# A decoder layer with a mixture of experts: the first expert's rows marked, listed, gathered and turned in two halves of 128, ahead of TensorE's loops

## The chip, the cores and the metric

One core of a Trainium2 chip runs one launch of the whole layer in float32. The time is the device time of that launch in microseconds. A profiled execution gives a page and a trace; other executions give the times.

## What is computed

The reference is one decoder layer: a combined attention mixer (latent attention and a forgetting attention side by side), a cross-attention to 256 memory tokens, a mixture of experts, and a last RMSNorm. Only the last but one bears on the change:

```python
xt = hn.reshape(T, D)                                   # T = 1024 tokens, D = 1024
logits = (xt @ w_router) + b_router                     # 32 experts
top_vals, top_idx = lax.top_k(logits, TOP_K)            # 4 of 32
gates = jax.nn.softmax(top_vals, axis=-1)
flat_e = top_idx.reshape(-1)
order = jnp.argsort(flat_e)
tok = order // TOP_K
xs = xt[tok]                                            # rows grouped by expert
h = lax.ragged_dot(xs, w_gate_up, group_sizes) + b_gate_up[e_sorted]
...                                                     # clamped SwiGLU
y = lax.ragged_dot(act, w_down, group_sizes) + b_down[e_sorted]
out = jax.ops.segment_sum(y * gate, tok, num_segments=T)
```

## The kernel before

The kernel is written per engine: each engine has its own stream of instructions, and semaphores order them. TensorE (PE) multiplies and transposes, VectorE (DVE) scales, adds and compares, ScalarE (ACT) does activations, GpSimd (POOL) issues the indirect DMAs, and SyncE (SP) issues the plain loads and stores.

**Router.** Tiles of 128 tokens pass the cross-attention and the router. For each, DVE picks the four largest logits and adds to `sel` (128 x 8 x 32, a 1 where a token has chosen an expert). After the last tile DVE raises `r_chosen` to SELECTED (1), PE multiplies ones and prefix matrices with the choices (`r_rank` 1 and 2), and DVE makes from this `key`, the place of each token within each expert's list. The experts are ordered by falling number of tokens. PE multiplies once more (`r_rank` 3), and DVE writes `items` (the expert of each place in the order, and its size) and `bounds` (how many experts are larger than each class width), and raises `r_chosen` to LISTED (3).

**Listing an expert.** For item i, DVE compares each tile's keys with a row of 256 numbers: eight instructions (`hots`, L2281) give `hot`, 128 x 8 x 256, a one-hot matrix from token to place. PE's `e_index` multiplies `hot` with `mv`, which holds each token's number in two parts, 8 products for places 0 to 127 and 8 for 128 to 255, into four columns of PSUM bank `pt[0]`. DVE's `indices` copies them (`ix`, L2287), adds the two parts to row numbers (`gidx`, L2290), raises `e_idx`, and forms the same numbers for the later scatter (`ixs`). Places beyond the expert's size get a number over the limit and are left out.

**Gathering.** POOL's `gather` (L955) waits for `e_idx` and issues two indirect DMAs of 128 rows of 4 KB, from the normed rows in HBM (`d_xn`) into `xg`; both count on `e_xg`.

**Turning in.** PE's `e_turn_in` waits for both halves (`e_xg` at 32 for item 0), and transposes `xg` in four groups g, each of four 128 x 128 blocks: two blocks of columns times two halves of rows. Groups use the banks `pt[0]` and `pt[1]` in turn; DVE's `x_copies` (L1938) scales each filled bank into `xe_t` and frees it, and raises `e_xt` after the last.

**PE's loops.** The experts fall into six classes by size (widths 256, 208, 184, 160, 144, 128), with one body of code for each. `up_to` (L1914 to L1924) nests five loops of two passes, each with a test `at < end` (loops L1916, tests L1917); `item` is the body. Only the number in `bounds` tells how many items a class has, so that an empty class is jumped over at run time. Each item begins with a test `at < 1` (L1909): item 0 alone runs its own turn-in there, as all later items are turned in by the item before. Then `whole` waits for `e_xt` and runs the products for gate and up (`e_gate_up`), the listing of the next item, the transposes of the last item's output, and the products for down. The kernel needs 32 items.

**Order around the change, PE:** wait for LISTED; load two item sizes and five bounds into registers (L1850, L1886), with `e_index(0)` between the third bound and the fourth; wait for ACT's biases (`r_ex` 3) and transpose them (eight blocks, L1892); set `at` to 0 (L1896); enter the loops; turn in item 0 inside the first item. **DVE:** load the first expert's number (L2277); `hots(0)`; `indices(0)`; gates (L2319 to L2326, `r_gate`); `x_copies(0)`; `hots(1)`; first item. **POOL:** `gather(0)`, then the splitting of the biases into three parts (L966 to L981), `gather(1)`, and the loop of shares, gathers and scatters. **SP:** loads the first weights (slot 0, 2 MB) once LISTED is reached; then waits for the gather (L769), stores the gates (L770), loads slot 1, waits for the store, and loads slots 2 to 5 (L603).

The lines in the profile are often those of helpers: L1376 is every product, L1760 the transposes of the turn-in, L603 every load. "DVEq" or "PEq" is an engine's sequencer, which runs branches, register work and waits.

Of the kernel before, what the change touches and what calls it, by code (L numbers as in the profile page):

```python
# [78 lines left out]
def build(nc, S, a, out):  # L79
    T, D, NT, KD, H, FW, E, CAP = S.T, S.D, S.NT, S.KD, S.H, S.FW, S.E, S.CAP  # L80
    ctx = ExitStack()
    with ctx:
        def sem(name):
            return ctx.enter_context(nc.semaphore(name))
# [362 lines left out]
        def index_use(i):  # L447
            return e_pt[0].base + 3 * i + 1
# [112 lines left out]
        def nothing():  # L561
# [5 lines left out]
            sem("r_ss"), sem("r_rstd"), sem("r_rnt"), sem("r_chosen"), sem("r_ex"), sem("r_rn"))  # L567
        SELECTED, PLACED, LISTED = 1, 2, 3
        r_st = sem("r_st")
        r_rank = sem("r_rank")  # L570

        e_w = [Handoff(sem, f"e_w{c}") for c in range(SLOTS)]
        e_hot = sem("e_hot")
        e_idx = sem("e_idx")
        e_xg = sem("e_xg")
# [12 lines left out]
        def apart(eng):  # L588


            eng.sem_inc(passed, 1)
# [9 lines left out]
        def _(sp):  # L601
# [165 lines left out]
            load(slots[0][:, :, :], expert_part(0, first), e_w[0].full)  # L767
            sp.wait_ge(e_xg, 32)
            sp.wait_ge(r_gate, 1)  # L769
# [41 lines left out]
        def _(po):  # L811
# [149 lines left out]
            po.wait_ge(r_ex, 1)  # L961
            gather(0)

# [401 lines left out]
        def _(pe):  # L1365
# [360 lines left out]
            def if_second(n, yes, no):  # L1726
# [5 lines left out]
                with pe.Else():  # L1732
                    no()

            def e_index(i, n=None):

                pe.wait_ge(e_hot, i + 1)

                pe.wait_ge(e_pt[0].free, index_use(i))

                def tokens(hb, tiles):
                    return product(pt[0][:, hb * 2:hb * 2 + 2],
                                   [(hot[:, t, hb * P:(hb + 1) * P], mv[:, t, :]) for t in range(tiles)])

                tokens(0, NT)
                if_second(n, lambda: tokens(1, NT).then_inc(e_pt[0].full, 1),
                          lambda: tokens(1, 1).then_inc(e_pt[0].full, 1))

            def e_turn_in(i, groups, n=None):

                pe.wait_ge(e_xg, 32 * (i + 1))
                for g in groups:
                    b, k = g % 2, g // 2 + 1
                    pe.wait_ge(e_pt[b].free, turn_in_use(b, i, k))

                    def blocks(halves):
                        for j in range(4):
                            if j % 2 in halves:
                                c = 2 * g + j // 2
                                m = pe.transpose(pt[b][:, j * P:(j + 1) * P], xg[:, j % 2, c * P:(c + 1) * P], ident)  # L1760
                        m.then_inc(e_pt[b].full, 1)

                    if_second(n, lambda: blocks((0, 1)), lambda: blocks((0,)))
# [118 lines left out]
            below = []  # L1882
            for c in range(S.CLASSES - 1):
                if c == 3:
                    e_index(0)
                below.append(pe.value_load(bounds[0:1, c:c + 1], min_val=0, max_val=E))  # L1886
            below.append(E)
            pe.wait_ge(r_ex, 3)
            for b in range(2):
                pe.wait_ge(e_rows[b].free, e_rows[b].base + 1)  # L1890
                for m in range(4 * b, 4 * b + 4):
                    x = pe.transpose(wide[1][0:BP, m * P:(m + 1) * P],  # L1892
                                     b_thrice[:, m, :], ident)
                x.then_inc(e_rows[b].full, 1)
            at = pe.alloc_register("item_at")
            pe.reg_mov(at, 0)  # L1896
# [3 lines left out]
            def item(w):  # L1900
# [7 lines left out]

                with pe.If_lt(at, 1):  # L1909
                    e_turn_in(0, range(4))  # L1910
                whole(i, i - 1, w, n_before, later, look_ahead)
# [23 lines left out]
        def _(ve):  # L1935
# [348 lines left out]
            def indices(i, e):  # L2284
# [5 lines left out]
                ve.scalar_tensor_tensor(out=gidx[:, :], **ids).then_inc(e_idx, 1)  # L2290
                ve.scalar_tensor_tensor(out=ixs[:, 0:2], **ids)
                ve.drain()
# [20 lines left out]
            first = expert_at(0)  # L2313
            hots(0, first)
            indices(0, first)
            ve.tensor_copy(ixp[:, :], ixs[:, :])

# [210 lines left out]
```

## Time and profile before

| | us |
|---|---|
| median of 3 runs | 2709.58 |
| lowest and highest run | 2707.89, 2711.74 |
| the profiled execution, its own time | 2707.28 |
| span of the profiled execution, first to last instruction | 2705.4 |

| engine | busy us | share | instructions |
|---|---|---|---|
| PE | 2638.0 | 98% | 17206 |
| DVE | 1091.5 | 40% | 2701 |
| ACT | 627.4 | 23% | 1386 |
| POOL | 379.9 | 14% | 391 |

The span is what the trace covers; 1.9 us of the execution lie outside it. All positions below are microseconds from the span's start. The mixer, cross-attention and router end at about 1070, and the 32 items of the expert stage fill the rest. A group of instructions in a timeline gives its start, the time that it covers, and in brackets how long the engine had been idle before it and what ended that. The profile counts one float32 product of the expert stage as two records, and a transpose as one.

### The profile page before, as it was taken

To read this page: it belongs to the slowest core of one execution; us is meant where nothing else is said; L and a number is where in the kernel's file an instruction comes from. 1 tells how busy PE (TensorE), PEld (TensorE's weight loads), DVE (VectorE), ACT (ScalarE), POOL (GpSimd) and SP (SyncE) were. 2 spreads that over 40 slices of the span, in tenths; PEclk is the share of its full clock that TensorE was granted. 3 is DMA by queue.
4 is the path that set the end of the run, shared out by engine and by line. 5 is a ranking of instruction groups with operands and counts; after the bars stand their busy time and mean duration, and the time that the engine had idled before them with its cause. 6 is when DMAs were issued, how large, how long until landed. Compare 5 with 4: busy or idle time off the path is not lost.

```text
span 2705.4 us, 49571 instructions
## 1 busy us (share of the span) xinstructions
PE 2638.0 (98%) x17206; PEld 2118.7 (78%) x17207; DVE 1091.5 (40%) x2701; ACT 627.4 (23%) x1386; POOL 379.9 (14%) x391
## 2 busy tenths in 40 slices
PE   9999999999999998999999999999999999999997
PEld 8455556666477774999999999998878787878785
DVE  1111145554212324433333344344455454545455
ACT  0333355553011112011111111111212121221212
POOL 0100022221000001111111111111111111112111
PEclk9999999999999998999999999999999999999998
DMA  8111243232300002765667677787888888888885
GB/s 293 47 51 54 64 151 90 79 116 92 129 1 9 31 31 103 303 209 194 221 218 254 225 276 260 269 274 264 318 299 319 301 310 306 312 297 312 300 310 202
DMA packets 108856, 533.95 MB, mean 197 GB/s; under 512 B 24290, under 2 KB 59042, under 8 KB 84208
## 3 DMA queue, kind: packets, MB, share of 16 engines
q1 hardware_dynamic: 88016, 498.99, 50.2%
q0 software_dynamic: 20768, 33.97, 5.7%
q8 instruction: 48, 0.79, 0.1%
q14 instruction: 24, 0.20, 0.0%
HBM read 506.64 MB, written 60.52 MB: 210 GB/s over the span
## 4 chain that ended last, share of the span: by engine, by line
PE 92%; DVE 3%; issue 2%; DMA 2%; ACT 1%; DVEq 1%; POOL 0%; ACTq 0%; POOLq 0%
PE bank L1376 45%; PE wide L1376 9%; PE wide L1836 9%; PE wide L1804 9%; PE bank L1426 8%; PE bank L1369 4%; PE wide L1500 2%; PE bank L1556 2%; PE bank L1760 2%; PE wide L1517 1%; DMA d_sum<-y_sb,sidx 1%; PE wide L1369 1%; DVE biased L2060 1%; DVE prob_t L2071 1%; ACT prob L1151 0%
## 5 line engine op out<-in xcount | busy, mean ns | idle before, releaser
L1376 PE MATMUL bank<-xe_t,slot 128*128 128x128 f32 (+4 forms) x8192 | 1025.2, 287 | 12.3 <-issue 11.2
L1376 PEld LDWEIGHTS bank<-xe_t,slot 128*128 128x128 f32 x8192 | 1014.5, 192 | 14.1 <-issue 13.7
L2336 DVE TENSOR_SCALAR glu<-bank,b_gu 128x256 f32<-128x256 f32 x256 | 123.8, 484 | 657.2 <-PE bank L1376 657.1
L1317 ACT ACTIVATE sig<-glu 128x256 f32<-128x256 f32 x256 | 106.7, 417 | 837.8 <-DVE glu L2336 835.5
L1836 PE MATMUL wide<-slot,act_t 128*128 128x512 f32 x608 | 267.8, 593 | 1.0 <-DVE act_t L2348 1.0
L1804 PE MATMUL wide<-act_t,slot 128*128 128x144 f32 (+3 forms) x1664 | 235.5, 302 | 0.0
L1804 PEld LDWEIGHTS wide<-act_t,slot 128*128 128x128 f32 x1664 | 231.8, 190 | 0.0
L1426 PE MATMUL bank<-w_in,xt 128*128 128x512 f32 (+1 forms) x512 | 217.6, 575 | 1.6 <-DVEq L1978 1.6
L1836 PEld LDWEIGHTS wide<-slot,act_t 128*128 128x128 f32 x608 | 112.5, 190 | 128.8 <-issue 126.2
L1334 ACT ACTIVATE y_t<-wide,b_dn 128x256 f32<-128x256 f32 x248 | 102.0, 471 | 421.2 <-PE wide L1836 212.9
L955 POOL DMA_INDIRECT xg<-d_xn,gidx x66 | 66.6, 1009 | 862.8 <-DVE gidx L2290 814.0
L1426 PEld LDWEIGHTS bank<-w_in,xt 128*128 128x128 f32 x512 | 94.8, 190 | 100.5 <-issue 100.5
L987 POOL DMA_INDIRECT share<-d_gate,sidx x64 | 67.8, 1059 | 458.6 <-DVEq L2357 415.4
L2348 DVE TENSOR_TENSOR act_t<-lin,sig 128x256 f32<-128x256 f32 x256 | 108.8, 425 | 41.0 <-issue 7.3
L1938 DVE TENSOR_TENSOR xe_t<-bank,gains 128x512 f32<-128x512 f32 x132 | 85.2, 686 | 96.8 <-PE bank L1760 91.6
L2338 DVE TENSOR_SCALAR lin<-bank,b_gu 128x256 f32<-128x256 f32 x256 | 121.6, 475 | 0.0
L2345 DVE TENSOR_TENSOR lin<-lin,glu 128x256 f32<-128x256 f32 x256 | 108.9, 425 | 19.4 <-issue 0.3
L1376 PEld LDWEIGHTS bank<-hn_t,w_xq 128*128 128x128 f32 x1024 | 115.5, 192 | 1.4 <-issue 1.1
L1376 PE MATMUL bank<-hn_t,w_xq 128*128 128x128 f32 x1024 | 115.7, 275 | 0.3 <-issue 0.3
L1376 PE MATMUL wide<-vw,px_t 128*128 128x512 f32 x256 | 112.4, 593 | 0.6 <-DVE lg_now L2171 0.6
L997 POOL DMA_INDIRECT d_sum<-y_sb,sidx x62 | 99.0, 1598 | 44.3 <-ACTq L1299 29.4
L1369 PE MATMUL bank<-const,prob 128*128 128x128 f32 x576 | 88.2, 281 | 11.6 <-DVE prob_t L2071 5.1
(302 smaller groups left out, 2455.6 us busy)
## 6 DMA issues: line engine op xcount, KB each, us to landing
slot<-in_w_gu SPq DMA_DIRECT2D x128, 2048.0 KB, 8.8
slot<-in_w_dn SPq DMA_DIRECT2D x64, 2048.0 KB, 7.7
w_in<-in_w_in SPq DMA_DIRECT2D x1, 6144.0 KB, 25.3
w_mem_k<-in_w_mem_kv SPq DMA_DIRECT2D x4, 1024.0 KB, 11.0
w_mem_v<-in_w_mem_kv SPq DMA_DIRECT2D x1, 4096.0 KB, 20.6
x_sb<-in_x SPq DMA_DIRECT2D x8, 512.0 KB, 3.3
cneg<-d_cneg SPq DMA_DIRECT2D x8, 512.0 KB, 6.6
d_vw<-mix_out SPq DMA_DIRECT2D x16, 256.0 KB, 2.2
```

Of the source, the lines that this page charges most:

```text
L997: po.indirect_dma_start(out=d_sum, out_offset=bass.IndirectOffsetOnAxis(ap=sidx[:, hb:hb + 1], axis=0), in_=y_sb[:, hb, :], in_offset=None ...
L1317: ac.activation(sig[m % 2][:, :], glu[m % 2][:, :], ACT.Sigmoid, scale=1.702).then_inc(e_sig, 1)
L1334: x = ac.activation(y_t[:, m, :], pp2[b][:, (m % 2) * CAP:(m % 2 + 1) * CAP], ACT.Identity, bias=b_dn[:, bass.ds(e * KD + m, 1)])
L1369: m = pe.transpose(dst[0:s.shape[-1], j * P:j * P + s.shape[0]], s, idn)
L1376: m = pe.matmul(dst, l, r_, start=(k == 0), stop=(k == n - 1))
L1426: m = pe.matmul(pp[b][:, 0:c1 - c0], xt[:, kk, :], w_in[:, kk, c0:c1], start=kk == 0, stop=kk == KD - 1)
L1804: x = pe.matmul(pp2[b][:, (m % 2) * CAP:(m % 2) * CAP + w], slots[4 + m // 4][:, k, (m % 4) * P:(m % 4 + 1) * P], act_t[:, k, 0:w], start= ...
L1836: x = pe.matmul(wide[1][:, hd * 512:(hd + 1) * 512], act_t[:, k, 0:P], slots[4 + hd][:, k, :], start=k == 0, stop=False)
L2336: ve.tensor_scalar(glu[b][:, :], pp[b][:, 0:CAP], b_gu[:, bass.ds(e * 2 * KD + 2 * m, 1)], 7.0, ALU.add, ALU.min).then_inc(e_glu, 1)
L2338: ve.tensor_scalar(lin[b][:, :], pp[b][:, CAP:2 * CAP], b_gu[:, bass.ds(e * 2 * KD + 2 * m + 1, 1)], 7.0, ALU.add, ALU.min).then_inc(e_gu[ ...
L2345: ve.tensor_tensor(lin[b][:, :], lin[b][:, :], glu[b][:, :], ALU.mult)
L2348: ve.tensor_tensor(act_t[:, m, :], lin[b][:, :], sig[b][:, :], ALU.mult).then_inc(e_act, 1)
```

## The change

The first item is taken out of the common path. DVE marks, copies and adds it in two halves of 128 places; PE multiplies the first half into bank `pt[1]` after its second bound (before: all after the third), and the second half into `pt[0]` after its third. POOL gathers each half once its numbers are there, on semaphores of their own (`e_half`, `e_xg`). PE transposes the first half of groups 0 and 1 when the first half has landed, the second half of both when the second has landed, then groups 2 and 3 as before, all in front of the loops and behind the bias transposes. The test `at < 1` and the turn-in go out of the items of all six classes. `r_chosen` gets two more steps and `r_rank` one. Waits for `e_xg` count 16 less for every item, since item 0's first half no longer counts there.

```diff
--- before.py
+++ after.py
@@ -565,12 +565,14 @@
         BIAS_ROWS = 2
         r_ss, r_rstd, r_rnt, r_chosen, r_ex, r_rn = (
             sem("r_ss"), sem("r_rstd"), sem("r_rnt"), sem("r_chosen"), sem("r_ex"), sem("r_rn"))
-        SELECTED, PLACED, LISTED = 1, 2, 3
+        SELECTED, PLACED, LISTED, HALF_HOT, HALF_LISTED = 1, 2, 3, 4, 5
+        HALF_MULTIPLIED = 4
         r_st = sem("r_st")
         r_rank = sem("r_rank")
 
         e_w = [Handoff(sem, f"e_w{c}") for c in range(SLOTS)]
         e_hot = sem("e_hot")
+        e_half = sem("e_half")
         e_idx = sem("e_idx")
         e_xg = sem("e_xg")
         e_y = Handoff(sem, "e_y")
@@ -765,7 +767,8 @@
             sp.wait_ge(r_chosen, LISTED)
             first = expert_of(0)
             load(slots[0][:, :, :], expert_part(0, first), e_w[0].full)
-            sp.wait_ge(e_xg, 32)
+            sp.wait_ge(e_half, 16)
+            sp.wait_ge(e_xg, 16)
             sp.wait_ge(r_gate, 1)
             sp.dma_start(d_gate.rearrange("(t p e) o -> p t (e o)", p=P, e=E), part[:, :, :]).then_inc(s_st, 16)
             load(slots[1][:, :, :], expert_part(1, first), e_w[1].full)
@@ -959,7 +962,19 @@
 
             po.wait_ge(r_st, 16 * NT)
             po.wait_ge(r_ex, 1)
-            gather(0)
+
+            def gather_half(hb, landed):
+                po.indirect_dma_start(
+                    out=xg[:, hb, :], out_offset=None, in_=d_xn,
+                    in_offset=bass.IndirectOffsetOnAxis(ap=gidx[:, hb:hb + 1], axis=0),
+                    bounds_check=T - 1, oob_is_err=False).then_inc(landed, 16)
+
+            po.wait_ge(r_chosen, HALF_LISTED)
+            apart(po)
+            gather_half(0, e_half)
+            po.wait_ge(e_idx, 1)
+            apart(po)
+            gather_half(1, e_xg)
 
 
 
@@ -1732,6 +1747,10 @@
                 with pe.Else():
                     no()
 
+            def tokens_of(bank_of, at_col, hb, tiles):
+                return product(bank_of[:, at_col:at_col + 2],
+                               [(hot[:, t, hb * P:(hb + 1) * P], mv[:, t, :]) for t in range(tiles)])
+
             def e_index(i, n=None):
 
                 pe.wait_ge(e_hot, i + 1)
@@ -1739,8 +1758,7 @@
                 pe.wait_ge(e_pt[0].free, index_use(i))
 
                 def tokens(hb, tiles):
-                    return product(pt[0][:, hb * 2:hb * 2 + 2],
-                                   [(hot[:, t, hb * P:(hb + 1) * P], mv[:, t, :]) for t in range(tiles)])
+                    return tokens_of(pt[0], hb * 2, hb, tiles)
 
                 tokens(0, NT)
                 if_second(n, lambda: tokens(1, NT).then_inc(e_pt[0].full, 1),
@@ -1748,7 +1766,7 @@
 
             def e_turn_in(i, groups, n=None):
 
-                pe.wait_ge(e_xg, 32 * (i + 1))
+                pe.wait_ge(e_xg, 32 * i + 16)
                 for g in groups:
                     b, k = g % 2, g // 2 + 1
                     pe.wait_ge(e_pt[b].free, turn_in_use(b, i, k))
@@ -1881,8 +1899,14 @@
 
             below = []
             for c in range(S.CLASSES - 1):
+                if c == 2:
+                    pe.wait_ge(r_chosen, HALF_HOT)
+                    pe.wait_ge(e_pt[1].free, e_pt[1].base + 1)
+                    tokens_of(pt[1], 0, 0, NT).then_inc(r_rank, 1)
                 if c == 3:
-                    e_index(0)
+                    pe.wait_ge(e_hot, 1)
+                    pe.wait_ge(e_pt[0].free, index_use(0))
+                    tokens_of(pt[0], 2, 1, NT).then_inc(e_pt[0].full, 1)
                 below.append(pe.value_load(bounds[0:1, c:c + 1], min_val=0, max_val=E))
             below.append(E)
             pe.wait_ge(r_ex, 3)
@@ -1892,6 +1916,20 @@
                     x = pe.transpose(wide[1][0:BP, m * P:(m + 1) * P],
                                      b_thrice[:, m, :], ident)
                 x.then_inc(e_rows[b].full, 1)
+            def turn_half(g, hb):
+                for j in (hb, hb + 2):
+                    c = 2 * g + j // 2
+                    m = pe.transpose(pt[g][:, j * P:(j + 1) * P], xg[:, hb, c * P:(c + 1) * P], ident)
+                return m
+
+            pe.wait_ge(e_half, 16)
+            for g in range(2):
+                pe.wait_ge(e_pt[g].free, turn_in_use(g, 0, 1))
+                turn_half(g, 0)
+            pe.wait_ge(e_xg, 16)
+            for g in range(2):
+                turn_half(g, 1).then_inc(e_pt[g].full, 1)
+            e_turn_in(0, (2, 3))
             at = pe.alloc_register("item_at")
             pe.reg_mov(at, 0)
             LEVELS = 5
@@ -1906,8 +1944,6 @@
                     pe.reg_mov(held, later)
                     pe.reg_mov(held_later, rows_in(i + 2))
 
-                with pe.If_lt(at, 1):
-                    e_turn_in(0, range(4))
                 whole(i, i - 1, w, n_before, later, look_ahead)
                 pe.reg_mov(at, i + 1)
 
@@ -2288,7 +2324,11 @@
                 ve.drain()
                 ids = dict(in0=ix[:, :, 0], scalar=float(8 * T), in1=ix[:, :, 1], op0=ALU.add, op1=ALU.add)
                 ve.scalar_tensor_tensor(out=gidx[:, :], **ids).then_inc(e_idx, 1)
-                ve.scalar_tensor_tensor(out=ixs[:, 0:2], **ids)
+                token_rows(e)
+
+            def token_rows(e):
+                ve.scalar_tensor_tensor(out=ixs[:, 0:2], in0=ix[:, :, 0], scalar=float(8 * T), in1=ix[:, :, 1],
+                                        op0=ALU.add, op1=ALU.add)
                 ve.drain()
                 ve.scalar_tensor_tensor(out=ixs[:, 2:4], in0=ixs[:, 0:2], scalar=float(E),
                                         in1=iota[:, bass.ds(e, 1)].to_broadcast([P, 2]), op0=ALU.mult, op1=ALU.add)
@@ -2311,8 +2351,28 @@
 
 
             first = expert_at(0)
-            hots(0, first)
-            indices(0, first)
+            def half_hots(hb):
+                for t in range(NT):
+                    ve.tensor_scalar(hot[:, t, hb * P:(hb + 1) * P], iota[:, hb * P:(hb + 1) * P], shift[:, 0:1],
+                                     key[:, t, bass.ds(first, 1)], ALU.add, ALU.is_equal)
+
+            def rows_of_half(hb):
+                return ve.scalar_tensor_tensor(out=gidx[:, hb:hb + 1], in0=ix[:, hb, 0:1], scalar=float(8 * T),
+                                               in1=ix[:, hb, 1:2], op0=ALU.add, op1=ALU.add)
+
+            half_hots(0)
+            ve.drain().then_inc(r_chosen, 1)
+            ve.wait_ge(r_rank, HALF_MULTIPLIED)
+            ve.tensor_copy(ix[:, 0, :], pt[1][:, 0:2])
+            ve.drain()
+            rows_of_half(0).then_inc(r_chosen, 1)
+            half_hots(1)
+            ve.drain().then_inc(e_hot, 1)
+            ve.wait_ge(e_pt[0].full, index_use(0))
+            ve.tensor_copy(ix[:, 1, :], pt[0][:, 2:4]).then_inc(e_pt[0].free, 1)
+            ve.drain()
+            rows_of_half(1).then_inc(e_idx, 1)
+            token_rows(first)
             ve.tensor_copy(ixp[:, :], ixs[:, :])
 
             ve.wait_ge(r_ex, 2)
```

## Rows read from the trace of the kernel before

**Rows 1.** The page: busy time and share, and the chain's shares by engine.

```profile
PE 2638.0 (98%) x17206; PEld 2118.7 (78%) x17207; DVE 1091.5 (40%) x2701; ACT 627.4 (23%) x1386; POOL 379.9 (14%) x391
...
PE 92%; DVE 3%; issue 2%; DMA 2%; ACT 1%; DVEq 1%; POOL 0%; ACTq 0%; POOLq 0%
```

**Rows 2.** Chain of waits in order of time: start us, us, what.

```profile
1076.83 0.58 PE bank L1376 x16
...
1078.94 1.43 POOL xg L955
...
1080.68 4.70 DMA xg<-d_xn,gidx
...
1090.61 47.43 PE bank L1376 x272
```

**Rows 3.** PE's sequencer by line: count, ns min/median/max, first and last start.

```profile
L1886 PEldq TENSOR_LOAD <-bounds x5: 295/306/309, 1074.8 to 1077.5; - x5
...
L1896 PEldq MOVE  x1: 35/35/35, 1078.3 to 1078.3; - x1
...
L1917 PEldq COMPARE_BRANCH  x1: 4747/4747/4747, 1078.5 to 1078.5; - x1
...
L1917 PEldq COMPARE_BRANCH  x7: 65/65/4747, 1078.5 to 1085.2; - x7
...
L1901 PEldq FUSED_REGOPS  x1: 111/111/111, 1085.4 to 1085.4; - x1
...
L552 PEldq COMPARE_BRANCH  x1: 4821/4821/4821, 2687.2 to 2687.2; - x1
...
L1901 PEldq FUSED_REGOPS  x1: 110/110/110, 1235.4 to 1235.4; - x1
...
L1909 PEldq COMPARE_BRANCH  x32: 78/209/350, 1085.5 to 2640.4; - x32
```

**Rows 4.** Timeline of SP at the gather's landing: start us, us, line, op.

```profile
1085.39 0.38 SPq L770 DMA_DIRECT2D d_gate<-part  x1
```

**Rows 5.** Timeline of DVE, 1066 to 1090.

```profile
1066.11 0.29 DVE L2187 TENSOR_TENSOR eq<-const,idxf 128x128 f32<-128x128 f32 x1
...
1073.90 2.67 DVE L2281 TENSOR_SCALAR hot<-const,shift,key 128x256 bf16<-128x256 f32 x8 [1.13 <-issue]
...
1077.70 0.16 DVE L2290 SCALAR_TENSOR_TENSOR gidx<-ix 128x2 int32<-128x2 f32 x1
...
1078.79 0.42 DVE L2319 TENSOR_TENSOR part<-part,sel 128x256 f32<-128x256 f32 x1
...
1089.64 0.69 DVE L1938 TENSOR_TENSOR xe_t<-bank,gains 128x512 f32<-128x512 f32 x1 [0.16 <-PE bank L1760]
```

**Rows 6.** Timeline of POOL; and all gathers of L955, issue to landing.

```profile
1078.94 1.43 POOL L955 DMA_INDIRECT xg<-d_xn,gidx  x1 [13.70 <-issue]
...
1080.68 0.99 POOL L955 DMA_INDIRECT xg<-d_xn,gidx  x1 [0.30 <-issue]
...
DMA to landing us min/median/max: 2.1/5.2/15.8
```

**Rows 7.** Timeline of PE: turn-in, first products of items 0 and 1.

```profile
1085.76 3.84 PE L1760 MATMUL bank<-const,xg 128*128 128x128 f32 x16 [5.55 <-DMA xg<-d_xn,gidx]
...
1090.61 13.17 PE L1376 MATMUL bank<-xe_t,slot 128*128 128x208 f32 x64 [1.01 <-DVEq L2305]
...
1162.13 11.42 PE L1376 MATMUL bank<-xe_t,slot 128*128 128x208 f32 x64
```

**Rows 8.** PE at a change of class; its waits for issue (total, times, longest).

```profile
1236.15 11.91 PE L1376 MATMUL bank<-xe_t,slot 128*128 128x184 f32 x64 [2.39 <-issue]
...
PE bank L1376 <- issue: 11.2, 4, 3.3
```

**Rows 9.** Windows: from:to us, busy PE, PEld, DVE, ACT, POOL, PEclk, DMA share, GB/s.

```profile
1090.00:1095.00 5.00, 4.39 (x16) 4.31 (x16) 4.14 (x7) 0.00 (x0) 3.39 (x3) 0.60 0.99 423
...
1237.00:1241.00 4.00, 4.00 (x17) 4.00 (x16) 0.00 (x0) 0.00 (x0) 0.00 (x0) 0.57 1.00 430
```

## The prediction

> **What bounds the kernel now.** The page comes first: PE is busy for 98% of the span, and 92% of the chain that ended last is PE [rows 1]. A microsecond taken from another engine counts only where PE stands still. The chain in order of time shows where that is around the change: between the router and the first expert product PE waits for a string of small steps, namely marking on DVE, 16 narrow products, the row numbers, the gather on POOL, its landing, 16 transposes and their copies, and at 1090.61 the first product [rows 2]. From there PE runs on, so what this stretch gains or loses is gained or lost at the end.
>
> The chain names the gather's landing as what PE waited for. The next view, PE's sequencer by source lines, says more. PE set its loop register (L1896) at 1078.3 and came to the item's own register work (L1901) at 1085.4, 7.1 us later, and the first transpose started at 1085.76 [rows 3, 7]. SP, which waits for the same landing, issued its store at 1085.39 [rows 4]. So **two things ended within 0.3 us of each other**: the gather, and PE's way into five nested loops. Of those 7.1 us one branch took 4747 ns: the first test of L1917, which jumps over the nest of the 256-wide class, empty here since the first products are 208 wide. PE's one other jump over a body that never ran (L552, at the end) took 4821 ns; the seven tests of L1917 at the entry have a median of 65 [rows 3]. I read the two as the price of a jump into code that was not at hand.
>
> **First half (marked, listed, gathered).** Eight markings of 256 columns take 2.67 us, so 0.32 apart from start to start; a 128-column DVE instruction is 0.13 shorter than a 256-column one (0.29 against 0.42) [rows 5]. Eight half markings: 8 x 0.19 = 1.5 us, done at 1075.5. PE is later: it now waits between its second and third load of a bound; the five loads began from 1074.8 to 1077.5, so some 0.68 apart, and two end at 1076.1 [rows 3]. Eight products instead of 16 (0.58, rows 2) take 0.4: 1076.6. The copy and the sum end 0.45 after the products (1077.41 to 1077.86 before) [rows 2, 5]: 1077.05, **0.8 earlier**. POOL starts a gather 1.08 after the row numbers end (1078.94) and its two took 1.43 and 0.99 [rows 6]: it starts at 1078.1 and ends by 1079.5.
>
> **Second half.** DVE marks it only after the first half's sums: 1077.05 + 1.5 + 0.1 = 1078.7, PE's eight products to 1079.15 (PE's third load is hidden beside the marking), row numbers at 1079.6, POOL 1.08 later at 1080.7. Before, it started at 1080.68 [rows 6]: **nothing gained**. This gather landed 4.7 after its start [rows 2], 1085.4 at the latest; the fastest of all 66 gathers took 2.1 [rows 6], 1082.8 at the earliest. It meets the weight load of slot 0 as before, but most of the first half is out of its way: I take 1085.1, near the nearest row.
>
> The Trainium skill (DMA: Bandwidth & Descriptors, "Anatomy of one DMA") has about 2.0 us plus bytes over 436 GB/s for such a transfer. For the second half's 57 to 80 rows of 4 KB that is an estimate of 2.6 us, a landing at 1083.3 and a sum 1.8 us lower than mine; the row above, 4.7, is far from it.
>
> **Turn-in.** Before, from 1085.73 to 1090.61: four groups of four transposes, 16 in 3.84 (about 0.21 apart, 0.42 each), each group followed by a copy of 0.69, two banks [rows 2, 5, 7]. After, half of groups 0 and 1 is done early, in idle time. From 1085.2: group 0 is full at 1085.85, its copy to 1086.55, group 2's transposes to 1087.7; group 1's copy to 1087.2, group 3's transposes start at 1087.5 and end at 1088.6, the last copy at 1089.35, drained 1089.4. Against 1090.38 **1.0 us earlier**.
>
> **Loop entry.** The turn-in now stands in front of the loops, so that PE's sequencer begins the entry only when group 3 can start, at 1087.4. The 7.1 us stood beside the gather before, and that cover is gone. What is left as cover is the copies, to 1089.4. 1087.4 + 7.1 = 1094.5, and from L1901 on a change of class takes 0.75 to the product (1235.4 to 1236.15), 0.48 without the removed branch [rows 3, 8]: **the first product at 1095.0, 4.4 us later than 1090.61**. With the landing at 1082.8 or 1085.4 this term is 2.1 or 4.7.
>
> The Trainium skill (Runtime: NRT & Kernel Launch, "Instruction fetch mechanics") says that a taken branch to a target outside the fetched window stalls until the page is fetched. It gives PE room for 2048 instructions, by which a jump over one item's body (under 900) might find its target; by that the entry would take about 2.4 instead of 7.1, and the sum would be that of the first rival. The 4747 ns argue against it here.
>
> **Removed branch.** Each item loses the test L1909 (median 209 ns, 32 times). Inside a class it costs nothing: PE's queue covers it (PE waited for "issue" four times only, all at changes of class [rows 8]); if that cover were gone it would come back with at most 0.27 an item. At the four changes of class PE stood still for 11.2 us in all, 2.39 at the first [rows 8]; there the branch and its step of 0.06 lie on the path, 4 x 0.27 = 1.1 by the median, 4 x 0.41 = 1.65 by the longest (350 ns): I take **1.35 us gained**, between the two.
>
> **Clock.** PE's clock was at its lower level, 1.2 GHz, until about 1094.0, 3.4 us into the products; that cost 13.17 - 11.42 = 1.75 us over the first 64 product records against the same ones of the next item [rows 7, 9] (the mean of 0.60 from 1090 to 1095 is 4 us at a half and 1 at full). PE will now stand some 6 us between transposes and products instead of 1.0. Bounds: the slow part as short as 2.5 us (-0.45) or twice as long (+1.75); I take +0.8, nearer the middle. Two of the four class changes were followed by such a dip, the one at 1237 stands in [rows 9], about 1.7 each: none or four afterwards, 3.4 either way, taken as 0.
>
> **At nothing:** the eight bias transposes (L1892) move 2 us later into PE's wait for the gather, and ACT's copies and POOL's bias work behind them; first wanted by item 0's sixth step, 30 us on. DVE's token rows and gates end at some 1082.4, while SP waits for the gather until 1085. POOL's new wait has only the gathers behind it. SP's store and slots 1 to 5 go out 0.3 earlier; slot 1 is wanted 12 us after the first product, and the loads keep that margin.
>
> **Sum:** +4.4 - 1.35 + 0.8 = **+3.85 us**. The profiled execution took 2707.28, 2.3 below the median of 2709.58; from it 2711.1, by the median **2713.4**. A measurement of this kernel tells some 0.2%, 5.4 us, from no change, so this is likeliest "same".
>
> **Rivals.**
> *No stall at the new place* (0.17). For it: the first change of class leaves and enters five levels within the 2.39 us of its gap and PE's queue. Against: both jumps of the trace over a body never run stalled alike. Entry 7.1 - 4.7 = 2.4; the first product at 1090.3, and -0.3 - 1.35 gives -1.65, with no clock term: 2707.9.
> *A second stall, slower* (0.15). Place: between the turn-in and the first product. The weight loads of slots 1 to 5 now run at full rate when the code is fetched, or the 208-wide entry starts near the end of a fetched piece. Price: one more 4.75, so +8.6, 2718.2. It decides once the entry takes over 8.7 us instead of 7.1.
> *The intended gain* (0.05): early landing at 1082.8 and no stall: the first product about 1088, -2.6 - 1.35 = -4: 2705.6. Against it: the second gather starts no earlier.
>
> My forecast has 0.63, its own range 2710.5 to 2717. Over 5.4 slower: all but a little of the second rival and 0.14 of my own case (clock, landing at the late end): 0.28. Over 5.4 faster needs the third rival or the first, with both dips gone: 0.05. Range 2706.5 to 2718.5: from the first rival less its spread to the second with its own.
>
> **What would show it.** L1917's first test at over 4 us, but now behind the last transposes, and PE's idle row before the first 208-wide product at about 5.5 us, released by "issue". The first gather starting near 1078.1, the second near 1080.7. Gaps at class changes shorter by 0.3 each. I am wrong if that first test takes under 1 us, if the idle row names the DVE copies, or if the second gather lands before 1083.5.

## The result, and the profile after

| | before | changed |
|---|---|---|
| median, us | 2708.38 (20 runs) | 2712.57 (20 runs) |
| lowest and highest run | 2704.89, 2711.74 | 2709.47, 2714.71 |
| span of the profiled execution | 2705.4 | 2711.7 |

The ratio is 1.0014, 95% interval 1.0008 to 1.0020: the changed kernel is 4.2 us slower by the medians, 2.2 to 5.4 by the interval. 2713.4 had been forecast.

Positions in two executions can only be compared from a common event, since the router in front ended 3.3 us later in the profiled execution of the changed kernel, and in the profiled executions of the kernels below it ended anywhere between 1072.6 and 1076.2. I count from LISTED, the end of DVE's write of `bounds`. Timeline of DVE, before:

```profile
1072.62 0.15 DVE L2273 CAST bounds<-wide 128x5 int32<-128x5 f32 x1
```

and after, with the two half markings:

```profile
1075.89 0.15 DVE L2309 CAST bounds<-wide 128x5 int32<-128x5 f32 x1
...
1077.18 2.14 DVE L2356 TENSOR_SCALAR hot<-const,shift,key 128x128 bf16<-128x128 f32 x8 [1.14 <-issue]
...
1080.14 2.46 DVE L2356 TENSOR_SCALAR hot<-const,shift,key 128x128 bf16<-128x128 f32 x8
```

LISTED is at 1072.77 before and at 1076.04 after. The first half's eight markings took 2.14 us, the second half's 2.46; all eight whole ones took 2.67 [rows 5]. Timeline of POOL, the gathers (2 lines), and of SP, the store that goes out on the landing:

```profile
1081.30 1.28 POOL L967 DMA_INDIRECT xg<-d_xn,gidx  x1 [12.80 <-issue]
...
1084.42 0.98 POOL L967 DMA_INDIRECT xg<-d_xn,gidx  x1 [1.83 <-DVE gidx L2360]
```

```profile
1088.78 0.38 SPq L773 DMA_DIRECT2D d_gate<-part  x1
```

From LISTED the first gather starts at 5.26 (before 6.17), the second at 8.38 (7.91), and the landing shows at 12.74 (12.62) [rows 4, 6]. The gather in halves brings the rows in no earlier. What comes next stands in the chain of waits in order of time:

```profile
1084.42 4.29 DMA xg<-d_xn,gidx
...
1088.75 0.70 PE bank L1922 x2
...
1090.32 1.96 PE bank L1778 x8
...
1092.29 0.69 DVE xe_t L1974
...
1093.04 6.82 issue
```

The copies end at 1092.98, and then there are 6.82 us of "issue", in which PE's engine waits for nothing but its own sequencer. The sequencer's lines, with the columns of [rows 3]:

```profile
L1934 PEldq MOVE  x1: 35/35/35, 1090.8 to 1090.8; - x1
...
L1953 PEldq COMPARE_BRANCH  x1: 6334/6334/6334, 1091.0 to 1091.0; - x1
...
L1953 PEldq COMPARE_BRANCH  x7: 65/65/6334, 1091.0 to 1099.3; - x7
...
L1939 PEldq FUSED_REGOPS  x1: 133/133/133, 1099.5 to 1099.5; - x1
```

The register before the loops (L1934, L1896 before) is set at 1090.8, behind the turn-in. The first test (L1953, L1917 before) takes 6334 ns against 4747 [rows 3], the item begins at 1099.5, and the first product at 1099.87. PE's timeline, first products and the four changes of class:

```profile
1099.87 13.94 PE L1391 MATMUL bank<-xe_t,slot 128*128 128x208 f32 x64 [7.61 <-issue]
...
1245.82 10.24 PE L1391 MATMUL bank<-xe_t,slot 128*128 128x184 f32 x64 [2.05 <-issue]
...
1376.05 8.96 PE L1391 MATMUL bank<-xe_t,slot 128*128 128x160 f32 x64 [2.41 <-issue]
...
1547.40 9.77 PE L1391 MATMUL bank<-xe_t,slot 128*128 128x144 f32 x64 [2.78 <-issue]
...
1856.54 7.41 PE L1391 MATMUL bank<-xe_t,slot 128*128 128x128 f32 x64 [2.37 <-issue]
```

Against 17.84 us after LISTED [rows 7], the first product comes at **23.83: 6.0 later**. Its 64 records take 13.94 instead of 13.17 [rows 7]. The gaps at the changes of class are 2.05, 2.41, 2.78 and 2.37. Before, the first was 2.39 [rows 8] and the others were these:

```profile
1368.52 8.96 PE L1376 MATMUL bank<-xe_t,slot 128*128 128x160 f32 x64 [2.87 <-issue]
...
1540.37 9.78 PE L1376 MATMUL bank<-xe_t,slot 128*128 128x144 f32 x64 [3.28 <-issue]
...
1850.02 7.41 PE L1376 MATMUL bank<-xe_t,slot 128*128 128x128 f32 x64 [2.70 <-issue]
```

The sum falls from 11.24 to 9.61. The page's product row says the same of the wait for "issue", first before, then after:

```profile
L1376 PE MATMUL bank<-xe_t,slot 128*128 128x128 f32 (+4 forms) x8192 | 1025.2, 287 | 12.3 <-issue 11.2
...
L1391 PE MATMUL bank<-xe_t,slot 128*128 128x128 f32 (+4 forms) x8192 | 1024.2, 287 | 17.2 <-issue 17.2
```

Idle time for "issue" went from 11.2 to 17.2 us: 7.6 new ones before the first product, 1.6 fewer at the changes of class. Windows of the changed kernel behind the first and the third change (the third number from the end is the granted clock):

```profile
1245.82:1249.82 4.00, 4.00 (x26) 4.00 (x27) 0.00 (x0) 0.00 (x0) 0.00 (x0) 1.00 0.86 336
...
1547.40:1551.40 4.00, 4.00 (x21) 4.00 (x22) 0.00 (x0) 0.00 (x0) 0.00 (x0) 0.64 0.95 410
```

Behind the third change the clock fell to its lower level for 3.4 us, as before; behind the first it did not, where before it had [rows 9].

Ledger from LISTED: +5.98 to the first product, +0.77 for slower first products, -1.63 at the changes of class, and -1.67 because the records after the first change took 10.24 instead of 11.91 [rows 8], at the higher clock: +3.45. From LISTED to the end the two executions differ by 3.0, so 0.4 us are not accounted for.

### The profile page after: what moved, and what is told of

Its sections match the earlier page's. It is cut to its first block, busy times and chain, and to the rows that moved or that the text cites. A ratio compares the mean times of both kernels' runs of the same rounds, so it can differ in the third digit from the quotient of the medians.

```text
span 2711.7 us, 49522 instructions
## 1 busy us (share of the span) xinstructions
PE 2640.4 (97%) x17206; PEld 2119.7 (78%) x17207; DVE 1097.2 (40%) x2711; ACT 627.8 (23%) x1386; POOL 380.1 (14%) x391
## 4 chain that ended last, share of the span: by engine, by line
PE 93%; DVE 3%; issue 2%; DMA 1%; ACT 1%; DVEq 1%; ACTq 0%; POOL 0%; POOLq 0%
PE bank L1391 46%; PE wide L1391 9%; PE wide L1854 9%; PE wide L1822 9%; PE bank L1441 8%; PE bank L1384 4%; PE wide L1515 2%; PE bank L1571 2%; PE bank L1778 1%; PE wide L1532 1%; PE wide L1384 1%; DVE biased L2096 1%; DMA d_sum<-y_sb,sidx 1%; DVE prob_t L2107 0%; ACT prob L1166 0%
## 5 line engine op out<-in xcount | busy, mean ns | idle before, releaser
L1391 PE MATMUL bank<-xe_t,slot 128*128 128x128 f32 (+4 forms) x8192 | 1024.2, 287 | 17.2 <-issue 17.2
```

Source lines behind the costliest of these rows:

```text
L1391: m = pe.matmul(dst, l, r_, start=(k == 0), stop=(k == n - 1))
```

## The experiments

Theory A: the loss is the entry into the loops, with its jump over the empty class, which lost the gather as its cover. Theory B: the halving costs, with its second marking, second wait and second gather. Each time is against runs of the kernel before on the same chip. "Product" is the first product after LISTED in the profiled execution. "Low stretches" counts, in the same execution, the stretches of some 3.4 us behind a change of class in which the granted clock was at its lower level, 1.2 GHz.

| run | product, us | first 64 records | low stretches | median us | before | ratio, 95% interval |
|---|---|---|---|---|---|---|
| before | 17.84 | 13.17 | 2 | 2708.38 | | 1 |
| changed | 23.83 | 13.94 | 1 | 2712.57 | 2708.38 | 1.0014 (1.0008 to 1.0020) |
| hoist_only | 24.68 | 13.74 | 1 | 2711.89 | 2708.70 | 1.0009 (1.0000 to 1.0018) |
| turn_inside | 20.77 | 13.73 | 2 | 2710.08 | 2708.70 | 1.0004 (0.9995 to 1.0013) |
| before_no_empty | 17.65 | 13.65 | 2 | 2708.00 | 2708.70 | 0.9996 (0.9987 to 1.0005) |
| after_no_empty | 17.10 | 14.05 | 1 | 2704.15 | 2708.70 | 0.9985 (0.9976 to 0.9994) |
| loads_later | 21.44 | 13.44 | 1 | 2707.69 | 2708.30 | 0.9995 (0.9986 to 1.0004) |
| hoist_no_empty | 17.10 | 11.52 | 1 | 2704.58 | 2708.30 | 0.9986 (0.9977 to 0.9995) |
| two_paths | 17.91 | 13.79 | 1 | 2704.80 | 2708.30 | 0.9986 (0.9977 to 0.9996) |
| jump_first | 18.88 | 13.14 | 2 | 2708.35 | 2708.30 | 1.0001 (0.9992 to 1.0010) |
| two_empty | 35.63 | 13.26 | 1 | 2723.99 | 2708.74 | 1.0055 (1.0041 to 1.0068) |
| hoist_two_paths | 17.69 | 13.08 | 1 | 2704.75 | 2708.74 | 0.9985 (0.9976 to 0.9994) |

The two kernels of the change have 20 times each, the runs 11, two_empty 5.

**The low stretches follow the removed test.** The four kernels that keep a test at each change of class, in the items or in front of the nests, stand still there for 10.87 to 11.32 us in all and have two such stretches; the eight without it stand still for 9.59 to 9.66 us and have one. Each stretch costs 1.67 us over the 64 records behind the change (11.91 against 10.24 behind the first, 10.63 against 8.96 behind the second, 9.77 against 8.10 behind the third). With one profiled execution of each kernel this is a clean split of twelve; no run changes the gaps and nothing else, so why one stretch goes is not shown.

### hoist_only: one part of the change, on the kernel before

```diff
+            e_turn_in(0, range(4))
             at = pe.alloc_register("item_at")
...
-                with pe.If_lt(at, 1):
-                    e_turn_in(0, range(4))
```

> The kernel before with one edit: item 0's turn-in, whole and not in halves, stands in front of the loops, and the test at < 1 goes out of the items. Theory A (the loop entry with its jump over the empty class lost its cover): the jump starts only when the last group can be transposed, some 15.4 us after LISTED (in the kernel before 5.7), takes 4.7 to 6.3 us, and the first product comes 5 to 7 us later than before; the class changes give 1.4 to 1.6 back and the clock costs 0.8: 4.5 to 6.5 us slower than before. Theory B (the loss comes from the halving, with its second marking and second gather, and the hoist is what gains): faster than before by 1 to 2 us.

Timeline and sequencer of PE (the whole loop nest's first test is listed under L1916 here):

```profile
L1916 PEldq COMPARE_BRANCH  x1: 6339/6339/6339, 1089.4 to 1089.4; - x1
...
1098.28 13.74 PE L1376 MATMUL bank<-xe_t,slot 128*128 128x208 f32 x64 [7.95 <-issue]
```

Without any halving the jump takes 6339 ns and the product comes 6.8 us later than before; the median is 3.2 us up, less than the 4.5 to 6.5 expected: the missing low stretch, 1.7 us, was not in that sum. Theory B said faster, and it falls. The product is 0.9 us later than in the changed kernel: the jumps are alike (6339 and 6334 ns), so the halves seem to save that much here.

### turn_inside: the changed kernel without the hoist

```diff
                 with pe.If_lt(at, 1):
+                    pe.wait_ge(e_half, 16)
+                    ...                        # the turn-in in halves, as in the change
+                    e_turn_in(0, (2, 3))
                 whole(i, i - 1, w, n_before, later, look_ahead)
```

> The changed kernel with the turn-in (in halves) and the test at < 1 back inside the first item; listing and gathering stay in halves. Theory A: the jump starts once the second half's products and the last two bounds are through, 8.0 us after LISTED, and the entry's 7.1 us end at some 15.3, after the landing at 12.6; the turn-in starts there, first product 19.8 to 20.2 us after LISTED (before 17.8, changed 23.8): 2 us slower than before, and 1.5 to 3 faster than the changed kernel. Theory B: as slow as the changed kernel or slower, since the halves are kept and the tests come back.

PE: the jump, the last two groups of the turn-in, the first products.

```profile
L1954 PEldq COMPARE_BRANCH  x1: 4536/4536/4536, 1084.5 to 1084.5; - x1
...
1091.61 1.94 PE L1922 MATMUL bank<-const,xg 128*128 128x128 f32 x8 [5.41 <-issue]
...
1096.95 13.73 PE L1391 MATMUL bank<-xe_t,slot 128*128 128x208 f32 x64 [1.01 <-DVEq L2346]
```

The jump starts 8.3 us after LISTED, takes 4536 ns, and the product is at 20.77, between the two kernels: 2.9 us later than before, because the second half's products and two bounds now stand in front of the loops, and 3.1 earlier than with the hoist. The median (1.4 us up, 2 expected) fits the trace in sign; its interval includes no change, and the profiled execution was the slowest of its 11.

### before_no_empty and after_no_empty: the jump taken away

```diff
-    S.CLASSES = 6
+    S.CLASSES = 5
...
-        WIDTHS = [P, 144, 160, 184, 208, CAP]
+        WIDTHS = [P, 144, 160, 184, 208]
```

Both leave out the 256-wide class, and so the case of an expert with more than 208 tokens.

> The kernel before with the empty 256-wide class taken out of PE's list of classes (five bodies; the 208-wide one comes first), so that nothing is jumped over. The output is the same for these inputs, and would not be for an expert with more than 208 tokens. Theory A: in the kernel before the jump ended together with the gather, so this gains only 0.3 us at the turn-in and whatever the clock does: within 1.5 us of before. Theory B (the jump is what bounds before too): several us faster.

> The changed kernel with the empty 256-wide class taken out in the same way. Theory A: the sequencer needs 2 us instead of 8.5 from the turn-in to the first product, so that the product waits for the last copy instead: 6 us earlier, some 17.5 us after LISTED; 5.5 to 7.5 us faster than the changed kernel and 1 to 3 us faster than before. Theory B: the changed kernel's time less 0.5 us, since the jump is hidden anyway.

The first products of before_no_empty:

```profile
1090.97 13.65 PE L1376 MATMUL bank<-xe_t,slot 128*128 128x208 f32 x64 [1.01 <-DVEq L2305]
```

and of after_no_empty:

```profile
1090.55 14.05 PE L1391 MATMUL bank<-xe_t,slot 128*128 128x208 f32 x64 [1.01 <-DVEq L2345]
```

In both the product is released by DVE's drain of the copies (DVEq), no longer by "issue". In the kernel before the jump was worth 0.2 us, in the changed one 6.7 us. With the jump gone, the change is a gain: 4.5 us below the kernel before and 3.85 below before_no_empty, by medians taken on the same chip; 1 to 3 below the kernel before was expected. Little of the gain is an earlier product. Between the traces of before_no_empty and after_no_empty the product is 0.55 earlier, its first 64 records 0.40 slower, the gaps at the changes of class 1.67 shorter and one low stretch of 1.68 gone, 3.5 of the 3.9 us from LISTED to the end. These two runs carry the verdict for theory A.

### loads_later: what makes the jump longer

```diff
+            sp.wait_ge(e_hot, 2)
             load(slots[1][:, :, :], expert_part(1, first), e_w[1].full)
```

> The changed kernel, where SP waits for DVE's marking of item 1 (e_hot at 2, some 23 us after LISTED) before it loads slots 1 to 5; in the changed kernel they go out 13.7 to 17 us after LISTED, beside the jump. If the 6.3 us of the jump are 4.5 to 4.8 plus waiting behind these loads (theory C), the jump takes 4.5 to 4.9, the first product comes 1.5 us earlier, and the time falls by 1 to 2 us (slot 1 lands some 9 us after its issue, before its first use). If the length comes from where the jump stands in the code and not from the loads (theory D), it stays at 6.3 and the time is the changed kernel's.

```profile
L1954 PEldq COMPARE_BRANCH  x1: 3855/3855/3855, 1090.9 to 1090.9; - x1
...
1097.31 13.44 PE L1392 MATMUL bank<-xe_t,slot 128*128 128x208 f32 x64 [5.16 <-issue]
```

The jump takes 3855 ns, 2.5 us less than in the changed kernel, and the product comes 2.4 earlier. Theory C holds, and its size was underrated: 3.9 is less than in the kernel before. The chapter on the hardware shows what the jump waits for. The time fell by more than the trace explains (4.8 us by the medians, each against its own runs of before; 2.2 from LISTED to the end of the two traces); the two ratios' intervals leave room for 2.2.

### hoist_no_empty: are the halves worth anything

Its edits are those of hoist_only and of before_no_empty together.

> The kernel before with the hoist alone and the empty 256-wide class taken out: the changed kernel's place of the turn-in without the halves and without the jump. Against the run after_no_empty it shows what the halves are worth once the jump is gone. By the traces: landing about the same (12.6 and 12.8 us after LISTED), turn-in 4.9 instead of 4.3 us long: first product 17.6 to 17.9 after LISTED instead of 17.1, 0.5 to 0.8 us slower than after_no_empty, still 3 to 4 us faster than before. If the halves carry the gain: as slow as before_no_empty.

```profile
1091.14 11.52 PE L1376 MATMUL bank<-xe_t,slot 128*128 128x208 f32 x64 [1.08 <-DVEq L2304]
```

The product stands at 17.10, as in after_no_empty, and the medians are 2704.58 and 2704.15. Once the jump is gone the halves can't be told from nothing. The product was expected 0.5 to 0.8 later than in after_no_empty, and part of why it was not is the clock: in this execution it was back at the higher level, 2.4 GHz, before the first product, the 16 transposes took 3.57 us instead of 3.84 [rows 7], and the first records 11.52.

```profile
1090.00:1095.00 5.00, 3.92 (x23) 3.87 (x23) 4.14 (x5) 0.00 (x0) 4.34 (x4) 1.00 1.01 419
```

### two_paths and hoist_two_paths: the jump out of the way for any sizes

```diff
-            for c, w in enumerate(reversed(WIDTHS)):
-                up_to(below[c], w, LEVELS)
+            def classes_from(c0):
+                for c, w in enumerate(reversed(WIDTHS)):
+                    if c >= c0:
+                        up_to(below[c], w, LEVELS)
+
+            with pe.If(below[0] < 1):
+                classes_from(1)
+            with pe.Else():
+                classes_from(0)
```

> The changed kernel with two copies of the loops: one If on the first bound; where it is below 1 (no expert over 208 tokens) the nests from 208 down stand right behind it, and the Else has all six. It computes the reference for any sizes. Theory A: the way to the first product holds no jump to far code, first product 17.1 to 17.5 us after LISTED, and the time is that of after_no_empty, 4 to 5 us faster than before; a far jump over the Else comes behind the last item, where PE has nothing left. Rival: the If stalls as the jump did, and the time stays the changed kernel's.

```profile
1091.93 13.79 PE L1391 MATMUL bank<-xe_t,slot 128*128 128x208 f32 x64 [1.01 <-DVEq L2352]
```

> The kernel before with the whole turn-in in front of the loops (no halves) and the two copies of the loops behind an If on the first bound. It computes the reference for any sizes. If the halves are worth nothing once the jump is gone, its time is that of two_paths within 1 us, 3.5 to 4.5 us faster than before; if the halves are worth the 0.5 us that the turn-in is shorter by, it is that much slower than two_paths.

```profile
1090.25 13.08 PE L1376 MATMUL bank<-xe_t,slot 128*128 128x208 f32 x64 [1.04 <-DVEq L2311]
```

Both are 3.5 to 4.0 us faster than before and, by the ratios, some 7.6 to 7.9 faster than the changed kernel, at the price of a second copy of five nests. The If itself did not stall. They beat both kernels, and the one without halves is the simpler. Against before, the product hardly moved (17.69 and 17.91, 17.84 before): in hoist_two_paths the gaps are 1.65 us shorter and one low stretch of 1.68 is gone, 3.3 of the 3.8 us from LISTED to the end.

### jump_first: the jump back under its cover

```diff
             for c, w in enumerate(reversed(WIDTHS)):
+                with pe.If_lt(at, 1):
+                    with pe.If_lt(at, below[c]):
+                        turn_first()           # the turn-in in halves, taken from in front
                 up_to(below[c], w, LEVELS)
```

> The changed kernel with the turn-in (in halves) between the class nests instead of in front of all: in front of each nest stands a test whether item 0 begins there, so that the jump over the empty nest is taken while the gather runs. The items stay without their test. Theory A: the jump begins 8.1 us after LISTED and takes 4.5, the turn-in starts at 13.4 and the first product comes at 18.3 to 18.8: 5 us earlier than in the changed kernel; the tests in front of the nests give back 0.3 at each class change. 4 to 5 us faster than the changed kernel, and level with before or up to 1 faster. Rival: no better than the changed kernel, since the five-level entry behind the turn-in is what costs.

```profile
L1945 PEldq COMPARE_BRANCH  x1: 3348/3348/3348, 1082.1 to 1082.1; - x1
...
1092.18 13.14 PE L1391 MATMUL bank<-xe_t,slot 128*128 128x208 f32 x64 [1.01 <-DVEq L2350]
```

The jump is taken while the gather runs, and the product comes 4.9 us earlier than in the changed kernel. The time is level with before: the gaps at the changes of class are 2.31 to 3.10, so part of what the removed test had given is back, and so is the second low stretch. The rival, that the five-level entry costs, falls.

### two_empty: the suspected cost twice

```diff
-        WIDTHS = [P, 144, 160, 184, 208, CAP]
+        WIDTHS = [P, 144, 160, 184, 208, 232, CAP]
```

> The changed kernel with a seventh class of width 232 between 208 and 256. It is empty too, so that the suspected cost stands there twice: two bodies to jump over instead of one. Theory A: a second jump of 3.9 to 6.3 us and 0.8 for its loop, the first product at 28.5 to 31 us after LISTED (changed: 23.8), 4.5 to 7 us slower than the changed kernel, 9 to 11 slower than before. Rival: one stall covers both bodies (the second jump finds its target), 1 us slower than the changed kernel.

PE: the two jumps, the last register work before the item, and the first products.

```profile
L1953 PEldq COMPARE_BRANCH  x1: 6464/6464/6464, 1091.0 to 1091.0; - x1
...
L1953 PEldq COMPARE_BRANCH  x1: 7099/7099/7099, 1098.5 to 1098.5; - x1
...
L1939 PEldq FUSED_REGOPS  x1: 137/137/137, 1107.7 to 1107.7; - x1
...
1111.86 13.26 PE L1391 MATMUL bank<-xe_t,slot 128*128 128x208 f32 x64 [20.41 <-issue]
```

The second empty body costs a second jump of 7099 ns. The product is at 35.63, 11.8 later than in the changed kernel, and the median is up by 15.3 over before: more than expected. Of the 11.8, 7.1 are the jump and 0.9 its loop. From L1939's start at 1107.7 to the product at 1111.86 it is 4.1 us, 0.4 in the changed kernel: another 3.7. There is no branch there, and the copies had long ended, so the sequencer stood still once more in straight code. The DMA view of the standstill, 1107.9 to 1111.6, has a packet of an instruction queue in it:

```profile
q8 instruction: 1, 0.02, 1.7%
```

## Why the prediction was right, point by point

The time (2713.4 against 2712.57, and +3.85 against +4.2) and its mechanism came as said: the entry into the loops lost its cover, and the jump came behind the turn-in. But the jump was priced too low and a term put at nothing was not nothing, and it was luck that the two errors nearly cancelled. The difference is also better resolved than the prediction thought: it put the limit at 5.4 us, and with 20 runs of each the interval, 2.2 to 5.4, does not reach down to no change.

- **First half.** 0.8 earlier was predicted, 0.9 measured.
- **Second half.** "Nothing gained" was 0.5 lost. The step that failed is 8 x 0.19 = 1.5 us for eight half markings. They took 2.14 (and 2.46 beside the gather's issue), 0.26 apart. The 0.13 had been taken from a tensor-tensor instruction; the marking itself shrank by 0.06 to 0.07 in spacing.
- **Landing.** 1085.1 was taken, 12.3 after LISTED; it was 12.74. The gather took 4.29 from its start, near the row of 4.7, and far from the 2.6 of the Trainium skill's formula (DMA: Bandwidth & Descriptors, "Anatomy of one DMA"): the measurement decides.
- **Turn-in.** Last copy 1.0 earlier predicted. From LISTED it ended at 16.94, 17.56 before: 0.6.
- **Loop entry.** L1896 behind the last group, at 14.6 after LISTED by the prediction and 14.8 measured. The first product, +4.4 predicted and +6.0 measured: the term was mis-sized by the jump, 6334 ns in place of 4747. The rest of the entry came as worked out, 2.3 us against 2.4, and the idle row before the first product is 7.61 instead of 5.5. That the price of the jump carries over from its old place to the new one was the weak assumption; the second rival had named the weight loads as a reason, but priced it as a whole second stall and not as 1.6 us. The entry took 8.7 us (1090.8 to 1099.5), just at the mark above which the prediction gave the case to that rival: so its reason had a part in the loss, through one longer jump and not through two.
- **The Trainium skill's rule** (Runtime: NRT & Kernel Launch, "Instruction fetch mechanics") is a stall at a taken branch whose target lies outside the fetched window. The traces agree in kind: the first jump over a body stalled in all seven kernels that have one near the turn-in. The Trainium skill's room for 2048 instructions, by which the target might have been at hand, did not help here.
- **Removed branch.** -1.35 predicted, -1.63 measured: each gap is 0.33 to 0.50 shorter.
- **Clock.** +0.8 predicted, +0.77 measured over the first 64 records. How far chance can move that term shows in hoist_no_empty, whose first records took 11.52. The other step that failed is the two later dips, "taken as 0": one was gone (-1.67), and hardly by chance, since all eight kernels without the test have one dip and all four with it have two. The removed branch and what went with it were worth 3.3 us, not 1.35.
- **At nothing.** SP's loads at nothing was wrong in one way: they were not late, but they ran at full rate beside the jump and made it longer (loads_later).

So the sum's errors, +1.6 at the jump, -0.3 at the branches and -1.7 at a dip, nearly cancel, though the first has nothing to do with the others. The median of 20 runs is a fair test only of the whole.

## What to carry to other kernels

An engine's sequencer has a critical path of its own: before work is moved, look at what its branches and register loads did beside the wait that the chain names; here two waits ended within 0.3 us of each other, and moving the work behind the one uncovered the other. A jump over a body that does not run belongs under a wait, or out of the usual path: with two copies of the loops the same hoist is 4 us faster than before instead of 3 us slower. Once that was done, the halving, which was most of the edit, was worth nothing that could be measured. And look where a gain comes from: of these 4 us the earlier start of the products, which the change was made for, gave 0.15, and 3.3 went with the small test that left each item.

## What the runs showed of the hardware that was not expected

**A far jump waits for a packet of code, and its price follows the DMA traffic of the core.** The windows below are those of the jumps (columns as in [rows 9]; the last number is GB/s).

Windows of loads_later during its jump of 3855 ns:

```profile
1090.90:1094.80 3.90, 1.25 (x6) 0.85 (x4) 2.44 (x3) 0.00 (x0) 3.49 (x5) 0.50 0.02 4
```

Of jump_first, 3348 ns:

```profile
1082.10:1085.50 3.40, 1.21 (x6) 0.75 (x4) 0.81 (x3) 1.87 (x3) 1.85 (x3) 0.50 0.55 175
```

Of turn_inside, 4536 ns:

```profile
1084.50:1089.00 4.50, 1.70 (x8) 1.22 (x6) 1.23 (x4) 2.47 (x3) 2.27 (x4) 0.50 0.48 158
```

Of the kernel before, 4747 ns:

```profile
1078.50:1083.25 4.75, 1.71 (x8) 1.22 (x6) 1.69 (x6) 2.47 (x3) 3.68 (x4) 0.50 0.83 299
```

Of the changed kernel, 6334 ns:

```profile
1091.00:1097.40 6.40, 1.26 (x6) 0.85 (x5) 4.94 (x5) 0.00 (x0) 5.47 (x6) 0.50 0.94 369
```

Of hoist_only, 6339 ns:

```profile
1089.40:1095.70 6.30, 0.93 (x5) 0.53 (x3) 5.16 (x7) 0.00 (x0) 4.91 (x4) 0.50 0.98 403
```

Of the second jump of two_empty, 7099 ns:

```profile
1098.50:1105.60 7.10, 0.00 (x0) 0.00 (x0) 0.49 (x2) 0.00 (x0) 0.00 (x0) 0.50 1.02 425
```

Near 0 to 175 GB/s a jump took 3.3 to 4.5 us, near 300 GB/s 4.75, and at 370 to 425 GB/s 6.3 to 7.1. The three low ones are not in order among themselves, and the jumps differ in place. loads_later changed the traffic at the same jump, and shows the cause.

What the jump waits for stands in the DMA view. The page of the changed kernel lists a queue of the kind "instruction", q8, with 48 packets of 16 KB (0.79 MB) in the whole launch. The one packet that any queue moved during the jump of loads_later is of it:

```profile
DMA packets 1, 0.02 MB, mean 4 GB/s; under 512 B 0, under 2 KB 0, under 8 KB 0
...
q8 instruction: 1, 0.02, 2.3%
```

and during the jump of the changed kernel there is again just one of it, beside 158 of the queue of plain loads and stores:

```profile
q1 hardware_dynamic: 158, 2.34, 93.3%
...
q8 instruction: 1, 0.02, 0.9%
```

By the traces' record of single packets, us:

| jump | from its start to the packet's | packet | from the packet's end to the jump's |
|---|---|---|---|
| jump_first, 3348 ns | 1.03 | 0.96 | 1.36 |
| loads_later, 3855 ns | 1.06 | 1.43 | 1.37 |
| turn_inside, 4536 ns | 1.70 | 1.48 | 1.36 |
| before, 4747 ns | 2.39 | 0.98 | 1.38 |
| changed, 6334 ns | 4.00 | 0.97 | 1.36 |
| hoist_only, 6339 ns | 4.00 | 0.96 | 1.38 |
| two_empty, second, 7099 ns (last of two packets) | 3.89 | 1.82 | 1.38 |

The end is the same within 0.02 us in all seven, and 1.35 to 1.53 in all 22 jumps of over 3 us that the twelve traces hold, each with its packet. What the traffic lengthens is mostly the time before the packet starts, 1.0 to 4.0 us, and in the second jump of two_empty the packet too. In the five kernels without an empty class on the way no packet of q8 moves between 1080 us and the first product, and no test there takes long.

**Straight code can stall too:** the 3.7 us in two_empty came without a branch. The packet of q8 in them runs from 1109.15 to 1110.14, 1.5 us before the sequencer goes on.

**Half the columns is not half the time:** a marking of 128 columns was spaced 0.26 us from the next, one of 256 columns 0.32.
